# Up projection of a two-layer block: 256 tokens walked through in other orders, chunk by chunk

## The reference, cut to what matters

```python
# x: (1, 256, 2048), w_up: (2048, 8192), w_down: (8192, 2048)
hm = rms_norm(x, g_mlp[i])
x = x + jnp.square(jax.nn.relu(hm @ w_up[i])) @ w_down[i]
```

## Time and profile before

| | us |
|---|---|
| median of 2 runs | 2662.61 |
| lowest, highest | 2660.84, 2664.37 |
| the profiled execution, its own time | 2664.01 |
| its span, first to last instruction | 2662.2 |
| mean granted TensorE clock | 0.996 of full speed |

### The profile page before, as it was taken

The page is one execution under the profiler, slowest core; times in us unless marked ns, Lnnn a source line. Parts: engine busy times, 40 slices in busy tenths (PEclk is TensorE's granted clock), DMA queues, the critical chain, the costliest instruction groups (busy, mean ns, idle before and its releaser), DMA issues.

```text
span 2662.2 us, 52796 instructions
## 1 busy us (share of the span) xinstructions
PE 2640.7 (99%) x22474; PEld 2591.6 (97%) x22474; DVE 1775.5 (67%) x2594; ACT 1337.8 (50%) x1817; POOL 112.5 (4%) x76
## 2 busy tenths in 40 slices
PE   9999999999999999999999999999999999999998
PEld 9998899899999999999899999999999999999997
DVE  7787779675555555565787786556676656665666
ACT  6474575554344443444445774444455435543553
POOL 2000021010000000000000000000300000000003
PEclk9999999999999999999999999999999999999999
DMA  7544546466666566665554556665566666666663
GB/s 254 181 143 151 177 157 189 150 207 192 196 192 197 191 195 193 196 192 178 166 167 153 178 180 194 194 195 183 150 199 192 196 193 196 192 196 192 197 191 103
DMA packets 137179, 488.45 MB, mean 183 GB/s; under 512 B 15344, under 2 KB 18288, under 8 KB 136944
## 3 DMA queue, kind: packets, MB, share of 16 engines
q1 hardware_dynamic: 136656, 484.82, 57.8%
q10 hardware_dynamic: 288, 0.26, 0.0%
HBM read 482.93 MB, written 2.10 MB: 182 GB/s over the span
## 4 chain that ended last, share of the span: by engine, by line
PE 94%; DVE 4%; ACT 1%; issue 0%; DMA 0%; SPq 0%; POOL 0%; ACTq 0%; DVEq 0%
PE ps L830 93%; DVE WL L1891 1%; PE ps L833 1%; DVE XL L1899 1%; DVE xT L1891 1%; DMA raw<-in_w_in 0%; ACT WH L1325 0%; DVE T L1891 0%; DVE XL L1891 0%; ACT xT L1325 0%; DVE T L1899 0%; DVE small L1899 0%; SPq L783 0%; DVE AL L1899 0%; ACT XH L1325 0%
## 5 line engine op out<-in xcount | busy, mean ns | idle before, releaser
L1891 DVE TENSOR_TENSOR WL<-raw,WH 128x1024 fp32r<-128x1024 f32 (+1 forms) x910 | 1123.6, 1238 | 755.2 <-ACT WH L1325 754.7
L1325 ACT ACTIVATE WH<-raw 128x1024 fp32r<-128x1024 f32 (+1 forms) x910 | 961.7, 1058 | 1265.0 <-PE ps L830 1261.9
L830 PE MATMUL ps<-XH,WH 128*128 128x256 f32 x5024 | 1401.2, 279 | 5.7 <-DVE WL L1891 3.6
L830 PE MATMUL ps<-XL,WH 128*128 128x256 f32 x5024 | 1389.5, 277 | 0.0
L830 PE MATMUL ps<-XH,WL 128*128 128x256 f32 x5024 | 1389.5, 277 | 0.0
L830 PEld LDWEIGHTS ps<-XH,WH 128*128 128x128 f32 x5024 | 943.1, 188 | 13.0 <-issue 11.6
L830 PEld LDWEIGHTS ps<-XL,WH 128*128 128x128 f32 x5024 | 943.3, 188 | 2.0 <-issue 1.2
L830 PEld LDWEIGHTS ps<-XH,WL 128*128 128x128 f32 x5024 | 942.9, 188 | 0.3
L830 PE MATMUL ps<-AH,WH 128*128 128x256 f32 x1856 | 513.0, 276 | 0.6 <-DVE AL L1891 0.4
L830 PE MATMUL ps<-AL,WH 128*128 128x256 f32 x1856 | 512.3, 276 | 0.0
L830 PE MATMUL ps<-AH,WL 128*128 128x256 f32 x1856 | 512.3, 276 | 0.0
(11 more groups left out here) (235 smaller groups left out, 1587.0 us busy)
## 6 DMA issues: line engine op xcount, KB each, us to landing
raw<-in_w_up SPq DMA_DIRECT2D x304, 512.0 KB, 4.3
raw<-in_w_in SPq DMA_DIRECT2D x223, 512.0 KB, 3.5
raw<-in_w_down SPq DMA_DIRECT2D x216, 512.0 KB, 4.3
raw<-in_w_out SPq DMA_DIRECT2D x64, 512.0 KB, 3.5
raw<-in_w_gates SPq DMA_DIRECT2D x64, 512.0 KB, 3.5
raw<-in_w_ckv SPq DMA_DIRECT2D x16, 512.0 KB, 3.6
raw<-in_w_cq SPq DMA_DIRECT2D x8, 512.0 KB, 4.4
raw<-in_w_co SPq DMA_DIRECT2D x8, 512.0 KB, 3.3
```

The source lines that it names most:

```text
L830: return e.matmul(out, l, r, start=start, stop=True, skip_group_check=True)
L1325: return e.activation(out, x, func, **kw)
L1891: return e.tensor_tensor(out, a, b, op)
```

## The change

A table `WALKS` gives an access pattern of the 256 token columns for seven of every eight `w_up` chunks (by c modulo 8; 0 has none). A pattern is a list of [step, count], outermost first. The new `walk` puts it on the moving operand and on the PSUM slice alike, so that column n of the result still belongs to token n, and every column is visited once. Nothing else is changed: the same matmuls in the same order, with the same weights, waits and signals.

```diff
+WALKS = {1: ([16, 8], [128, 2], [1, 16]), 2: ([2, 128], [1, 2]), 3: ([16, 16], [1, 16]), 4: ([2, 64], [128, 2], [1, 2]),
+         5: ([8, 16], [128, 2], [1, 8]), 6: ([32, 4], [128, 2], [1, 32]), 7: ([4, 64], [1, 4])}
...
+            def walk(x, job, c):
+
+                if job != "w_up" or c % 8 not in WALKS:
+                    return x
+                return bass.AP(x.tensor, x.offset, [x.ap[0], *WALKS[c % 8]])
+
...
                             for p, (w, o) in enumerate(passes):
-                                m = mm(to, tiles(w)[j][:, i, :], o[:, kt, :],
+                                m = mm(walk(to, job, c), tiles(w)[j][:, i, :], walk(o[:, kt, :], job, c),
                                        k == 0 and j % 2 == 0 and i == 0 and p == 0)
```

## The result

The changed kernel takes 2693.22 us (median of 2 runs, 2691.72 to 2694.72) against 2662.61 before: a ratio of **1.0115**, 95% interval 1.0099 to 1.0132. That is 30.6 us slower, within the 2% that I called no change and inside the stated range, but clear of noise. My likeliest case, no cost at all, did not come; the time is rival A's. What I expected the changed profile to show failed in two places: the round of chunks 4 to 7 did not stay at 87.04 us, and chunks 4 and 12 took over 28 us, which I had named as the sign of a failed prediction.

What follows compares the result with a forecast made beforehand. The prediction took TensorE's matmul stream to bound the kernel. Its four terms, 0 + 0 + 0 + 0 on the profiled 2664.0 us, 1.4 us above the median, gave 2663 us, with a range of 2653 to 2716 us.

Steps and rivals of the forecast that it cites:

- likeliest case: Walked w_up matmuls cost nothing extra: 2663 us, own range 2659 to 2668; chance 0.61.
- rival A: In walked w_up matmuls each run costs one clock period, 0.42 ns: +29 us, 20 in chunks 4 and 12; chance 0.15.
- The bound: TensorE, 99% busy and 94% of the chain, waits for nobody; matmul gains or losses enter the time one for one.
- Part 1: Three of the seven w_up patterns are built as plain order and cost 0; 1536 matmuls have a real walk.
- Part 2 and 4: Instructions, weights, DMAs and signals unchanged: 0; relu and multiplication read finished banks in plain order as before: 0.
- Part 3: Price of a walk in 1536 w_up matmuls: bounds -10 and +490 us, taken as 0 from the plain 256-column float32r matmul.
- The sign of being wrong: The prediction fails if any walked w_up chunk takes over 28 us; a chunk cost 21.76 us.
- The weighing: Skill's sentences on walked matmuls: one makes all 1536 pay, milder ones make all four walks free; no run decided.
- The reserve of 6.6 ns: A w_up matmul's 113.3 ns exceeds the full-clock 106.7 by 6.6 ns, said to cover some 16 jumps of 0.42 ns.
- B: All 1536 walked w_up matmuls are slow; at twice 113.3 ns, +174 us, 2837 us; chance 0.16.
- C: Walked w_up matmuls lose the fast float32r form and cost plain float32: +490 us, 3153 us; chance 0.03.
- D: A walk in w_up matmuls avoids what costs 6.6 ns: -10 us at most, 2653 us; chance 0.04.

Runs made afterwards that it cites:

- e4: Changed kernel with other walks on both operands: runs of 2 stepping by 64 to 4 columns, runs of 4 and 64 at 128; 2886.43 us.
- e1: Changed kernel with the four walks on the moving operand alone, PSUM written in plain order; 2692.67 us, ratio 1.0113.
- e2: Changed kernel with the four walks on the PSUM columns alone, moving operand read in plain order; 2662.48 us, ratio 1.0001.
- e7: Changed kernel with 15 other orders on the PSUM columns alone, moving operand plain; 2664.30 us.
- e8: Changed kernel with both operands of its eight really walked chunks going backwards in runs of two; 2670.50 us, ratio 1.0029.
- e6: Changed kernel with other orders on the moving operand alone, every column once, backwards or forward; 111.6 to 136.6 ns a matmul.

## Why the prediction was right, and where it was not

- **The bound.** Right. TensorE's stream sets the time one for one: 30.3 us in the unbroken piece, 30.6 in the median, and the waits behind it grew by as much as the round.
- **Part 1, the patterns that are none.** Right: chunks 2, 3 and 7 are at 113.3 ns. **Part 2 and 4**: right, nothing else moved.
- **Part 3, the price of a walk, taken as 0 from the nearest row.** This is the step that failed. That row was near in type, count and tile, and far in the one thing that the change alters, the sequence of addresses. The walks cost 55.7, 10.0, 7.0 and 6.0 ns a matmul. The chance of 0.61 for no cost rested on it. That the time still fell into the stated range is in part luck with the pattern: the range reached up to 2716 us for rival A's sake, and the change's runs of two alternate between two places only. With 4 to 64 places they cost twice as much, and e4 took 2886.43 us, far outside.
- **The sign of being wrong** (any walked chunk over 28 us) came with chunks 4 and 12, at 32.44 us. It did not fit my own range: rival A, which the range takes in, has these chunks 10 to 22 us above 21.76.
- **The reason I gave for 0**, that two neighbouring values stay together, is refuted for the read by e1, and true for PSUM by e2 and e7.
- **The weighing.** The sentence of the Trainium skill, page Advanced Engine Details and Errata, section Memory Cachelines, that any non-contiguous PSUM pattern slows matmuls, did not hold for pairs: 113.3 ns in 15 orders. Its milder neighbour, pairs kept together, did. From the part on SBUF, two hits on a line, I had taken that all four walks are free, and runs of two cost 169.1 ns. The rule fits these prices only if hits are counted on each of the two sides of theory W, where two columns in a row are one hit each; that reading is inferred.
- **Rival A** had the time nearly right, 29 us against 30.3, and that is mostly luck, since its mechanism, a fixed cost for each jump, is refuted by e8 (118.5 ns with 128 jumps). It split as 20.5, 5.1, 2.6 and 1.3 us for runs of 2, 8, 16 and 32; measured were 21.4, 3.8, 2.7 and 2.3. A jump is not worth 0.42 ns: it was worth 0.43, 0.31, 0.43 and 0.75 in the change, nothing in runs of 64, and in e4 the same 128 jumps cost twice as much. It also said that only chunks 4, 12 and, by a quarter, 5 would stretch; 6 and 1 did too. Its other form, runs of two at twice the price, is what e4 found with 4 to 64 places, but not a property of the run: backwards (e6, e8) runs of two cost 118.5 ns.
- **The reserve of 6.6 ns** that should cover sixteen jumps is none: eight jumps already showed. It is no limit of the weights either, since 111.6 ns was reached with the same weight loads.
- **B and C** did not come; B's 226.6 ns is real, but for walks that take one column per side from a line. **D** was right in kind: an order exists that wins 1.7 ns of the 6.6, only not among the change's.

Still open: why whole-line walks cost between 0 and 23 ns more, why four places of single columns cost 141.6, and what the remaining 5 ns over 106.7 are.

## What to carry to other kernels

Where the trace has no row with the property that a change alters, the nearest row in every other respect is weak evidence for zero; give the small-cost case more of the chance. In a kernel bound by its float32r matmuls, choose the order of columns for the moving operand's read: keep at least four neighbouring columns together, aligned to four (113 to 137 ns here), or take single columns in turns from two places; not runs of two that jump to another group of four, nor every second column, nor single columns from four places (141.6 ns). The order in PSUM was free in all orders tried, which kept pairs together, and the reader can undo an order with a strided read.

## What the runs showed that I had not expected

- Reading 0 128 1 129 costs 111.6 ns a matmul of 256 columns, less than 0 1 2 3 at 113.3; plain order shifted by one or two columns costs 120.0 and 120.7.
- Every second column, every third and every fourth cost the same, 228.3, 228.9 and 232.6 ns: twice the plain price is the ceiling for nearly all orders tried (243.3 was the highest).
- PSUM accumulates float32 pairs in any of 15 orders at 113.3 ns, and ScalarE (577 against 578 ns) and VectorE (688 against 688 ns) read every second column of it at no extra time.
